# A hybrid gated-branch trunk: the R and F gate projections in pieces between the steps of the state and retention loops

## What is computed

```python
def _retention_states(k, v, lg, r0):        # chunks of 128 tokens
    incr = einsum("bhncd,bhnce->nbhde", kc_ * zeta, vc_)
    step(r, u) = g_chunk * r + u, r         # scan over the chunks
def _retention_outputs(q, k, v, lg, r_prev):
    sc = einsum("bhncd,bhnmd->bhncm", q_, k_) * decay
    return einsum(sc, v_) + einsum(q_ * xi, r_prev)
y_r = head_norm(y)                          # y: the sum of both directions
y_f = fft2(px["f_u"]).real
def _merge(ys, zs, merge_logits, w_os, w_out):
    gates = sigmoid(merge_logits)
    total += gates[:, :, i] * ((ys[i] * silu(zs[i])) @ w_os[i])
    return total @ w_out
```

## Time and profile before

| | us |
|---|---|
| median of three runs | 2870.05 (2866.59 to 2872.36) |
| span of the profiled execution | 2869.4 |
| PE busy | 2636.5 (92%), 13096 matmul instructions |
| POOL busy | 1289.4 (45%) |
| DVE busy | 1148.2 (40%) |
| ACT busy | 1120.1 (39%) |

### The profile page before, as it was taken

One profiled execution on the slowest core, in us unless ns is written; L12 is line 12 of the kernel. 1 busy time (PEld: TensorE's weight loads), 2 busy tenths in 40 slices (PEclk: granted clock), 3 DMA queues, 4 the chain that ended last, 5 costly groups with the idle time before them and its releaser, 6 DMA issues.

```text
span 2869.4 us, 40066 instructions
## 1 busy us (share of the span) xinstructions
PE 2636.5 (92%) x13096; PEld 2155.5 (75%) x13096; DVE 1148.2 (40%) x2014; ACT 1120.1 (39%) x2337; POOL 1289.4 (45%) x1012
## 2 busy tenths in 40 slices
PE   7788959888999999999999869888999999999998
PEld 2788958766887778888887368767888778888886
DVE  2443455397243223324331354595244233333332
ACT  2644552476222433334332242575213333333332
POOL 1557952355222345556554132354221445555553
PEclk9889989999998899999999979999997999999999
DMA  5346641100120233344336431000120233344333
GB/s 226 87 120 186 189 153 59 30 1 6 48 62 24 57 94 111 109 127 149 112 109 230 152 107 48 19 1 20 45 62 14 81 99 109 110 132 143 110 109 121
DMA packets 387923, 270.53 MB, mean 94 GB/s; under 512 B 15452, under 2 KB 360668, under 8 KB 385252
## 3 DMA queue, kind: packets, MB, share of 16 engines
q1 hardware_dynamic: 373792, 231.26, 26.8%
q10 hardware_dynamic: 14024, 37.88, 3.7%
HBM read 259.63 MB, written 9.45 MB: 94 GB/s over the span
## 4 chain that ended last, share of the span: by engine, by line
PE 53%; issue 20%; POOL 14%; DVE 9%; ACT 3%; POOLq 1%; DMA 0%; DVEq 0%; SPq 0%; ACTq 0%
PE ps L568 52%; POOL w_lo L485 14%; DVE a_probT_lo L1275 2%; DVE a_q_split L1275 1%; DVE softmax_stats L1454 1%; DVE a_out_sum L1275 1%; PE ps L691 1%; ACT a_probT_hi L1061 1%; DVE norm_tmp L1355 1%; PE ps L604 1%; DVE hT_lo L1275 0%; DVE softmax_stats L1275 0%; ACT a_prob L1051 0%; DVE r_prev L1566 0%; DVE softmax_stats L1461 0%
## 5 line engine op out<-in xcount | busy, mean ns | idle before, releaser
L485 POOL TENSOR_TENSOR w_lo<-w_raw,w_hi 128x512 fp32r<-128x512 f32 x786 | 1051.7, 1345 | 1130.8 <-ACT w_hi L917 1120.8
L568 PE MATMUL ps<-hT_hi,w_hi 128*128 128x512 f32 (+1 forms) x2528 | 943.6, 373 | 47.4 <-POOL w_lo L485 22.0
L568 PE MATMUL ps<-hT_lo,w_hi 128*128 128x512 f32 (+1 forms) x2528 | 936.7, 371 | 0.0
L568 PE MATMUL ps<-hT_hi,w_lo 128*128 128x512 f32 (+1 forms) x2528 | 936.1, 370 | 0.0
L917 ACT ACTIVATE w_hi<-w_raw 128x512 fp32r<-128x512 f32 x786 | 493.6, 631 | 1088.6 <-PE ps L568 949.7
L568 PEld LDWEIGHTS ps<-hT_hi,w_hi 128*128 128x128 f32 x2528 | 485.8, 192 | 137.1 <-POOL w_lo L485 16.7
L568 PEld LDWEIGHTS ps<-hT_hi,w_lo 128*128 128x128 f32 x2528 | 485.4, 192 | 78.7
L568 PEld LDWEIGHTS ps<-hT_lo,w_hi 128*128 128x128 f32 x2528 | 486.0, 192 | 77.9
L1275 DVE TENSOR_TENSOR merge_tmp<-merge_tmp,ps 128x512 f32<-128x512 f32 (+1 forms) x160 | 101.5, 634 | 685.3 <-PE ps L568 613.2
L522 POOL TENSOR_TENSOR a_prob<-a_prob,softmax_stats 128x640 f32<-128x640 f32 (+2 forms) x144 | 163.4, 1135 | 177.5 <-DVE softmax_stats L1474 177.5
L1275 DVE TENSOR_TENSOR merge_tmp<-merge_tmp 128x512 f32<-128x512 f32 (+1 forms) x120 | 182.4, 1520 | 4.1
(11 more groups left out here) (187 smaller groups left out, 2972.3 us busy)
## 6 DMA issues: line engine op xcount, KB each, us to landing
w_raw<-in_w_in SPq DMA_DIRECT2D x512, 256.0 KB, 2.9
w_raw<-in_w_o_rest SPq DMA_DIRECT2D x120, 256.0 KB, 2.7
w_ada<-in_w_ada SPq DMA_DIRECT2D x16, 1536.0 KB, 9.2
w_raw<-in_w_out SPq DMA_DIRECT2D x80, 256.0 KB, 2.9
w_raw<-in_w_o_attn SPq DMA_DIRECT2D x40, 256.0 KB, 2.7
w_raw<-in_dft_x SPq DMA_DIRECT2D x32, 256.0 KB, 2.7
rope<-in_rope ACTq DMA_DIRECT2D x4, 1024.0 KB, 5.0
gate_row<-gate_rows ACTq DMA_DIRECT2D x5, 512.0 KB, 3.5
```

Of the source, the lines that this page charges most:

```text
L485: eng.tensor_tensor(w_lo[:, r, :], raw[:, r, :], w_hi[:, r, :].bitcast(F32), ALU.subtract).then_inc(sem["w_split"], tally.up("w_split"))
L568: return eng.matmul(dst, lhsT, rhs, start=start, stop=stop)
```

## The change

The order of tiles in a full pass becomes ... R_V, R_V+1, R_Z, R_Z+1, F_Z, F_Z+1, F_U, F_U+1, on every engine: SP loads F_Z's weights before F_U's. R_Z, R_Z+1, F_Z and F_Z+1 (`FILL`) are no longer issued by `project` but by a generator, `filler`, which yields after every six matmuls; a tile is eight such pieces in an image pass and four in a context pass. Four pieces stand before each turn of the values (two in a context pass), two in each step of `states` (four), one in each step of `retention` (two). The pieces write to banks 4 to 7 (`fill_bank`). For that, `states` moves to banks 0 to 3, and the scores have banks 0 and 1 alone: PE now waits for `sc` of step i before it issues the scores of step i+1. PE also waits for the last two `inc_saved` at the end of `states`, and for F_Z+1's evacuation before `turn_outputs`.

ACT evacuates R_Z behind the stage end, R_Z+1 in the middle of `states`, F_Z at its end, F_Z+1 behind the squares and before the root. POOL makes the `w_lo` of two units before the third `r_qx`. The two tiles of F_Z behind `fourier` are gone.

```diff
@@ -49,6 +49,7 @@
 Z_A, Z_B, Z_R, Z_F, ZT = 0, 4, 6, 8, 10
+FILL = (R_Z, R_Z + 1, F_Z, F_Z + 1)
 BRANCH = ((Z_A, 4), (Z_B, 2), (Z_R, 2), (Z_F, 2))
@@ -324,7 +325,7 @@
         for n, p in enumerate(passes):
-            p.tiles = list(range(MERGE)) if p.full else [A_K, A_V, R_K, R_K + 1, R_V, R_V + 1]
+            p.tiles = [*range(R_Z), *FILL, F_U, F_U + 1] if p.full else [A_K, A_V, R_K, R_K + 1, R_V, R_V + 1]
             for t in p.tiles:
@@ -369,6 +370,10 @@
             return z_pass[p.s][:, 0:p.NB, tile:tile + count, :]
+
+        def fill_bank(p, t):
+
+            return 6 - 2 * (tile_no[p.n, t] % 2)
@@ -468,9 +473,9 @@
                 tiles(l, A_Q + 2, F_U - 2)
+                tiles(l, F_Z, 2)
                 tiles(l, F_U, 2)
                 fourier(p)
-                tiles(l, F_Z, 2)
                 for b in range(p.NB):
@@ -529,6 +534,8 @@
                 for i, n in enumerate(outside_in(p)[::-1]):
+                    if i == 2:
+                        low_parts(first + 2 * R_Z + 6 + LOOK)
                     eng.wait_ge(sem["ret_y"], tally.take("ret_y"))
@@ -550,8 +557,9 @@
                     attention(p)
-                    low_parts(first + 2 * F_U + LOOK)
+                    low_parts(first + 2 * R_Z + 4 + LOOK)
                     retention(p)
+                    low_parts(first + 2 * R_Z + 6 + LOOK)
                 first += p.units
@@ -634,6 +642,28 @@
+            def filler(p):
+
+                for t in FILL:
+                    eng.wait_ge(sem["proj_out"], tally.take("proj_out"))
+                    for u in range(2):
+                        r = slot()
+                        for b in range(p.NB):
+                            at_ = slice(b * p.BW, (b + 1) * p.BW)
+                            for k in range(4):
+                                kk, w = 4 * u + k, slice(k * P, (k + 1) * P)
+                                last = three(ps[:, fill_bank(p, t) + b, 0:p.BW], w_hi[:, r, w], w_lo[:, r, w],
+                                             hT[0][:, kk, at_], hT[1][:, kk, at_], kk == 0, kk == KT - 1)
+                                if k == 3 and b == p.NB - 1:
+                                    last.then_inc(sem["w_used"], tally.up("w_used"))
+                                if k % 2:
+                                    yield
+
+            def fill_in(fill, parts):
+
+                for _ in range(parts):
+                    next(fill, None)
+
             def turn_values(p, t, before):
@@ -723,26 +753,29 @@
-            def states(p):
+            def states(p, fill=None):
                 order = outside_in(p)
...
                     for j in range(2):
-                        last = eng.transpose(ps[:, 4 + i % 2, j * P:(j + 1) * P],
+                        last = eng.transpose(ps[:, i % 2, j * P:(j + 1) * P],
                                              rk[:, j, order[i] * P:(order[i] + 1) * P], ident[:, :])
...
                         turn_keys(i + 1)
+                    if fill:
+                        fill_in(fill, 8 * p.NB // p.NT)
                     eng.wait_ge(sem["kz"], tally.take("kz"))
...
                         v = rv[:, n, h // 2, h % 2 * HD:h % 2 * HD + HD]
-                        last = mm(ps[:, 6 + i % 2, h * HD:(h + 1) * HD], r_kz[:, i % 2, h, :, :], v, True, True)
+                        last = mm(ps[:, 2 + i % 2, h * HD:(h + 1) * HD], r_kz[:, i % 2, h, :, :], v, True, True)
                     last.then_inc(sem["inc"], tally.up("inc"))
-
-            def retention(p):
+                eng.wait_ge(sem["inc_saved"], tally.now("inc_saved", 2))
+
+            def retention(p, fill):
                 order = outside_in(p)[::-1]
@@ -750,14 +783,15 @@
-                        last = mm(ps[:, i % 2 + 4 * (h % 2), h // 2 * P:(h // 2 + 1) * P], rk[rows, h // 2, c],
+                        last = mm(ps[:, h % 2, h // 2 * P:(h // 2 + 1) * P], rk[rows, h // 2, c],
                                   qd[rows, h, c], True, True)
...
                 for i, n in enumerate(order):
+                    eng.wait_ge(sem["sc"], tally.take("sc"))
                     if i + 1 < p.NT:
                         scores(i + 1)
-                    eng.wait_ge(sem["sc"], tally.take("sc"))
+                    fill_in(fill, 4 * p.NB // p.NT)
                     eng.wait_ge(sem["ret_qx"], tally.take("ret_qx"))
@@ -769,6 +803,7 @@
                 def turn_outputs():
+                    eng.wait_ge(sem["proj_out"], 2 + tile_no[p.n, F_Z + 1] + 1)
                     for b in range(p.NB):
@@ -877,16 +912,17 @@
                 project(p, 6)
+                fill = filler(p)
+                fill_in(fill, 2 * p.NB)
                 turn_values(p, R_V, A_V)
+                fill_in(fill, 2 * p.NB)
                 turn_values(p, R_V + 1, R_V)
-                project(p, 2)
                 stage_end(eng, tally, "pe")
-                states(p)
-                retention(p)
+                states(p, fill)
+                retention(p, fill)
                 pe_goes_on(eng, tally)
...
                 fourier(p)
-                project(p, 2)
                 pe_goes_on(eng, tally)
@@ -1003,7 +1039,7 @@
                 eng.wait_ge(sem["w_used"], tally.take("w_used__done", 2))
-                act(dst, banks(2 * (tile_no[p.n, t] % 2), p), func).then_inc(sem["proj_out"], tally.up("proj_out"))
+                act(dst, banks(fill_bank(p, t) if t in FILL else 2 * (tile_no[p.n, t] % 2), p), func).then_inc(sem["proj_out"], tally.up("proj_out"))
@@ -1099,9 +1135,15 @@
             def states(p):
+                if p.full:
+                    tile_range(p, FILL[0], FILL[0] + 1)
                 for i, n in enumerate(outside_in(p)):
                     eng.wait_ge(sem["inc"], tally.take("inc"))
-                    act(r_inc[:, n, :, :], ps[:, 6 + i % 2, 0:RH * HD].rearrange("p (h d) -> p h d", h=RH)).then_inc(sem["inc_saved"], tally.up("inc_saved"))
+                    act(r_inc[:, n, :, :], ps[:, 2 + i % 2, 0:RH * HD].rearrange("p (h d) -> p h d", h=RH)).then_inc(sem["inc_saved"], tally.up("inc_saved"))
+                    if p.full and i == p.NT // 2 - 1:
+                        tile_range(p, FILL[1], FILL[1] + 1)
+                if p.full:
+                    tile_range(p, FILL[2], FILL[2] + 1)
@@ -1128,6 +1170,7 @@
                     squares(i)
+                tile_range(p, FILL[3], FILL[3] + 1)
                 eng.wait_ge(sem["ret_var"], tally.take("ret_var"))
@@ -1239,13 +1282,12 @@
                     eng.dma_start(rope[:, :, :], a["rope"]).then_inc(sem["rope_in"], tally.up("rope_in", 16))
-                tile_range(p, R_Q, F_U)
+                tile_range(p, R_Q, R_Z)
                 stage_end(eng, tally, "act")
...
                 fourier(p)
-                tile_range(p, F_Z, MERGE)
                 stage_end(eng, tally, "act")
@@ -1579,7 +1621,7 @@
                     eng.wait_ge(sem["k_turned"], tally.take("k_turned"))
-                    k = ps[:, 4 + i % 2, 0:RH * HD].rearrange("p (h d) -> p h d", h=RH)
+                    k = ps[:, i % 2, 0:RH * HD].rearrange("p (h d) -> p h d", h=RH)
                     for d in range(2):
@@ -1613,7 +1655,7 @@
                         ins = tt(r_sc[:, i % 2, h::2, :],
-                                 ps[:, i % 2 + 4 * h, 0:2 * P].rearrange("p (j n) -> p j n", j=2), dt_[:, h::2, :])
+                                 ps[:, h, 0:2 * P].rearrange("p (j n) -> p j n", j=2), dt_[:, h::2, :])
                         ins.then_inc(sem["sc"], tally.up("sc")) if h else ins.then_inc(sem["dve_own"], tally.up("dve_own"))
@@ -1640,6 +1682,7 @@
                 fold(0)
+                placed(p, R_Z + 1)
                 for b in range(p.NB):
@@ -1653,7 +1696,7 @@
                 placed(p, F_Z + 1)
-                eng.wait_ge(sem["w_used"], tally.now("w_used__done", units_of(p)[0]))
+                eng.wait_ge(sem["w_used"], tally.now("w_used__done", units_of(p)))
                 for part in range(1 if p.ctx else 2):
@@ -1664,7 +1707,7 @@
-                return 2 * F_Z + (2 if p.ctx else 16), 2 * MERGE + (2 if p.ctx else 16)
+                return 2 * MERGE + (2 if p.ctx else 16)
@@ -1757,7 +1800,7 @@
                 fourier(p)
-                tally.skip("w_used__done", units_of(p)[1])
+                tally.skip("w_used__done", units_of(p))
                 stage_end(eng, tally, "dve")
```

## The result

The changed kernel takes 2842.53 us (median of four runs, 2836.18 to 2846.73) against 2871.20 for the kernel before on the same chip (2866.59 to 2874.29): ratio 0.9892, 95% interval 0.9879 to 0.9906. The forecast was 2832, the range 2818 to 2858. The direction and the range are right. The size was forecast too large: 28.7 us were won where 38.4 were forecast, and between the two profiled executions (spans 2869.4 and 2844.8) 24.6.

The account below looks back on a forecast made before the run. PE, busy 92% of 2869.4 us, was taken as the bound. Terms sum to 17.7 us per image pass, 35.4 for both, plus 3 for context: 38.4 less, 2831.0 profiled, 2832 as median; range 2818 to 2858.

Parts of the forecast that it names:

- The central step: Image passes' `retention` loop: with one piece per step the clock comes up to 1.00; 0.50 kept as the other end.
- The step that failed: Start of `retention` in image passes: scores 0, then a PE wait of 1.2 us (now 1.5) with nothing issued behind.
- rival 1: Retention loop's clock swings, half of the steps low at 3.3 us each: 2858 us (2845 to 2870); chance 0.11.
- I cost at nothing: POOL's two `w_lo` before the third `r_qxi`: no cost, as they finish before it may start; 2.7 us without that cover.
- `states`, without the stage end: Image pass's `states` loop with two pieces a step: own work 8.8 us against 12.4, gain 3.6.
- `retention` with F_U's lead-in: Image pass's `retention` loop with one piece a step: 36.8 us becomes 22.7, gain 14.1, nearly all of it clock.
- change-overs: Seams where runs of pieces are entered and left: 0.1 us for each of 30, loss 3.0 (0 to 8) a pass.
- Fourier and merge: Merge starts without the 1.1 us for F_Z+1's evacuation, its first weights 0.3 late: gain 0.8 a pass.
- The context pass: Two-step loops: steps gain about 4, merge 2, some 3 lost behind the loop; net gain 3, bounds 0 and 6.
- 2 (the clock stays down): One piece a retention step isn't enough, so wide matmuls run at the low clock: 2889 us, slower; chance 0.08.
- 3 (weights late): ACT splits the filler's units late, 0.8 each for eight a pass, 13 us: 2845; chance 0.08 together with rival 4.
- 4 (pieces fill nothing): Waits stay beside the pieces in the loops, 2 x 4.8, clock gain stays: 2842; chance 0.08 together with rival 3.

Follow-up runs that it names:

- bare loop: Changed kernel with all eight pieces between the first scores and the first wait for `sc`, none in the retention loop's steps: 2838.97 us in one execution.
- filled start: Changed kernel with two pieces issued behind the first scores in all passes, so the last two steps get none: 2825.5 us, ratio 0.9831.
- the run with the context pass filled alone: Changed kernel with two pieces behind the first scores in the context pass only: 2834.81 us, ratio 0.9864.
- the later F_Z: Changed kernel with F_Z's evacuation behind the second save of the outputs in image passes, POOL's two `w_lo` one step later: 2832.38 us in one execution.

## Why the prediction was right, and where its size was wrong

**The central step held.** "I take 1.00" for steps with a piece in them: where the loop had started well the clock stayed at 1.00 in every step with a piece, and in the bare loop it fell. The steps measure 3.96 us (2.05 + 0.58 + 1.36 = 3.99 forecast). The Trainium skill's rule on groups that cycle through PSUM banks (TensorE: Matmul & The Clock Gate, section "A second HAM failure mode: psum-queue depth-cycling") speaks of short idle times between such groups. In the filled start's steps there are none (PE busy 16.00 of 16.00 us, clock 1.00), so they don't test it; the bare loop, with waits of 0.4 and 0.9 us and a fall behind the second, is nearer to what it describes.

**The step that failed** is the start of `retention`. The prediction gave it "a wait of 1.2 (now 1.5)" and, in rival 1, even wrote that the clock "fell once in the loop's first microseconds behind the 1.5 wait for `r_scoresT`, a wait that stays", and then gave it a chance of 0.11, against rows that lie in the middle of a loop. The wait was 2.0, and 17.1 us of the loop in layer 1 and 13.7 in layer 0 ran at the low level. A step there takes 7.32 (4.76 + 1.36 x 0.427 / 0.227 = 7.3: the prices were right), so 17.1 us at the low level cost 17.1 x (1 - 3.96 / 7.32) = 7.8, and the two loops of the run with the context pass filled alone, alike but for the clock, differ by 7.9. The clock then came back by itself within the loop, which it had not done in 32 us without pieces.

**Why the wait was 2.0:** GpSimd's two `w_lo` "I cost at nothing". I had looked at what waits for them, and not at what they run beside. The first of them holds up one of VectorE's four scans for 1.0 us, so that the four take 1.9 instead of 0.9. In numbers that is the 0.8 between 1.2 and 2.0; that it decided the clock isn't shown (with the scans at 0.9 the clock stayed up in two loops of two, with them at 1.9 in one of six).

**The other terms** of layer 1's pass. Forecast 17.7; measured 13.5:

| Term | forecast | measured |
|---|---|---|
| turns of the values, with the stage end (1.5 - 0.3) | 1.2 | 1.3 |
| `states`, without the stage end | 3.6 | 3.4, then the 0.5 on `r_inc` |
| `retention` with F_U's lead-in | 14.1, less its seams | 6.0 |
| change-overs | -3.0 | about 0 |
| F_U | 1.0 | 0.9 |
| Fourier's head | 0 | 1.3 |
| Fourier and merge | 0.8 | 1.0 |

Two errors went the other way. **Change-overs**: a step of 3.96 leaves nothing for seams beyond what 2.05 holds. **Fourier's head**: behind F_U the clock fell once more in the kernel before and doesn't now (first row of before, second of after):

```profile
2242.00:2262.00 20.00, 15.10 (x54) 10.24 (x53) 6.83 (x10) 7.58 (x12) 2.65 (x3) 0.91 0.05 13
```

```profile
2237.00:2262.00 25.00, 19.12 (x82) 14.51 (x81) 6.82 (x10) 8.84 (x14) 5.64 (x5) 1.00 0.10 29
```

The version doesn't decide that fall alone: in the run with F_Z+1's evacuation earlier it came as well. With these two, 17.7 + 3.0 + 1.3 - 7.8 - 0.8 = 13.4, against 13.5 measured. That the forecast came so near is thus partly luck: without these two, 4.3 us in this pass, the gain would have been smaller still. With the filled start, 17.7 + 3.0 + 1.3 + 1.2 (no wait) = 23.2, against 717.94 - 694.99 = 22.95. F_U's `w_lo` came as foreseen: 0.7 at 2224.09. The longer wait at the stage end too (1.5 for 1.1).

**The context pass** was forecast at +3 within 0 to 6 and gave -4.75: outside its bounds. I had counted squares and splits behind its loop, and not its start, where the end of POOL's second `r_qxi` and both `w_lo` fall on the four scans (3.37 us), so that a loop of two steps begins with a wait longer than one of them. Context 4.75 + 3 = 7.8 and 4.2 and 2.0 less than forecast in the stretches of layer 1 and layer 0 make the missing 13.9 of the profiled executions; by the medians 9.7 are missing. One sum of the range is off as well: the parts named for its fast end give 2821, not 2819.

**Rivals.** 2 (the clock stays down), 3 (weights late) and 4 (pieces fill nothing) didn't come. Rival 1 came in part: the clock fell at the start, came back once and stayed; half of its mechanism, and in size close to what it said of low steps (3.3 each; measured 7.32 - 3.96 = 3.36). It put half of the steps at the low level; 17.1 and 13.7 us are four of sixteen.

**Open:** what decides whether the clock falls behind the 2.0 us wait (it didn't in one of six loops), whether the shorter wait of the later F_Z keeps it up or did so by chance, and whether in the bare loop the 0.9 us waits or the short passes let it fall.

## What to carry to other kernels

Work that is spread into a loop against waits should start before the loop's first wait, not after it: here one line at the start was worth about half as much again as the whole change (15 to 18 us beside 31, by the ratios), for the larger part because the clock didn't fall as the loop began. When an instruction is moved to an idle engine, ask what runs beside it and what that shares with it, not only who waits for it. And treat a pass with two trips through the loop apart from one with eight: it is nearly all start and end.

## What the runs showed of the hardware

- Four scans of 64x64 with two inputs in SBUF take 0.9 us alone and 1.9 to 3.4 beside GpSimd's 128x512 products. A scan that starts behind such a product lasts as long as the product, 1.3 us instead of 0.3.
- Steps of 24 short passes (128 and 64 columns) and six matmuls of 512 ran at 1.00 in all twelve image loops whose start was filled too, and in the changed kernel the clock came back from 0.50 in such steps after 14 to 17 us. In the kernel before, the short passes alone ran 32 us at 0.50 with the engine busy throughout.
- Where the clock falls isn't the same in two executions of the same code: the stretch of `retention` in layer 0 behind the same 2.01 us wait ran once at 0.51 and once at 1.00.
